# A hybrid decoder layer: the small on-chip tiles are allocated ahead of the staged block, not behind it

## The reference, cut to what matters

```python
h = x
proj = rmsnorm(h, norm_mix_g) @ w_in                      # 1024 -> 4624 columns
y_a  = gmlp_chunk_mixer(proj[..., :2048], ...)            # gelu, per-head norm, causal mixing in chunks of 128
y_b  = ssd_mixer(proj[..., 2048:], ...)                   # conv of 4 taps, silu, chunked state-space scan, gate, norm
h = h + concat([y_a, y_b]) @ w_out                        # 2048 -> 1024
hid = relu(rmsnorm(h, norm_mlp_g) @ w_ff1)                # 1024 -> 4096
h = h + (hid * hid) @ w_ff2                               # 4096 -> 1024
gate = sigmoid(rmsnorm(h, ple_norm_g) @ w_ple_gate)       # 1024 -> 1024
h = h + gate * (p @ w_ple_proj)                           # 256 -> 1024
out = rmsnorm(h, final_norm_g)
```

## Time and profile before

| what | value |
|---|---|
| median of 3 runs | 772.87 us (771.78 to 773.25) |
| the profiled execution, its own time | 771.78 us |
| its span, first to last instruction | 770.1 us |
| mean granted TensorE clock | 0.998 of full speed |
| busy share of the span: PE, PEld, DVE, ACT, POOL | 98%, 81%, 57%, 42%, 11% |
| moved by DMA | 81.88 MB, 106 GB/s over the span |

### The profile page before, as it was taken

The page is one execution under the profiler, slowest core; times in us unless marked ns, Lnnn a source line. Parts: engine busy times, 40 slices in busy tenths (PEclk is TensorE's granted clock), DMA queues, the critical chain, the costliest instruction groups (busy, mean ns, idle before and its releaser), DMA issues.

```text
span 770.1 us, 9090 instructions
## 1 busy us (share of the span) xinstructions
PE 757.4 (98%) x3492; PEld 623.7 (81%) x3492; DVE 436.1 (57%) x488; ACT 326.3 (42%) x456; POOL 87.4 (11%) x60
## 2 busy tenths in 40 slices
PE   8999999999999999999999999999999999999996
PEld 7888877887887888888888888888888888888885
DVE  5556894668569575547454443444444444446754
ACT  6525447645475812326443140413223140323556
POOL 1022210864562000000000000000000000000000
PEclk9999999999999999999999999999999999999999
DMA  9622323432422443123423232332323232332102
GB/s 334 191 83 83 109 79 119 133 109 87 161 82 83 144 157 136 42 69 108 127 93 110 82 110 96 95 107 84 109 82 109 82 100 96 102 120 82 47 0 110
DMA packets 35193, 81.88 MB, mean 106 GB/s; under 512 B 3924, under 2 KB 5592, under 8 KB 35160
## 3 DMA queue, kind: packets, MB, share of 16 engines
q1 hardware_dynamic: 33928, 77.20, 30.8%
q10 hardware_dynamic: 1232, 4.23, 1.7%
HBM read 79.28 MB, written 2.13 MB: 106 GB/s over the span
## 4 chain that ended last, share of the span: by engine, by line
PE 93%; DVE 3%; ACT 1%; issue 1%; DMA 1%; SPq 0%; ACTq 0%; DVEq 0%
PE acc L1122 29%; PE acc L1124 29%; PE acc L1123 29%; PE side L1184 3%; PE side L1277 2%; DVE w_lo L751 1%; PE side L1244 1%; DVE conv L948 1%; DMA gain<-in_norm_mix_g 1%; PE side L1284 1%; PE side L1272 1%; DVE h L937 0%; PE acc L1201 0%; ACT w_hi L431 0%; PE side L1224 0%
## 5 line engine op out<-in xcount | busy, mean ns | idle before, releaser
L1122 PE MATMUL acc<-w_hi,a_hi 128*128 128x512 f32 x512 | 204.2, 399 | 0.0
L1124 PE MATMUL acc<-w_hi,a_lo 128*128 128x512 f32 x512 | 199.7, 390 | 0.0
L1123 PE MATMUL acc<-w_lo,a_hi 128*128 128x512 f32 x512 | 199.3, 389 | 0.0
L431 ACT ACTIVATE w_hi<-w_raw 128x1024 fp32r<-128x1024 f32 (+1 forms) x128 | 130.2, 1036 | 145.5 <-PE acc L1124 143.3
L751 DVE TENSOR_TENSOR w_lo<-w_raw,w_hi 128x1024 fp32r<-128x1024 f32 (+1 forms) x128 | 166.1, 1298 | 45.0 <-ACT w_hi L431 44.3
L802 DVE TENSOR_TENSOR h<-h,acc 128x1024 f32<-128x1024 f32 x48 | 58.6, 1220 | 106.1 <-PE acc L1124 106.0
L1122 PEld LDWEIGHTS acc<-w_hi,a_hi 128*128 128x128 f32 x512 | 96.2, 188 | 21.0 <-issue 1.4
L1123 PEld LDWEIGHTS acc<-w_lo,a_hi 128*128 128x128 f32 x512 | 96.2, 188 | 20.7 <-issue 1.4
L1124 PEld LDWEIGHTS acc<-w_hi,a_lo 128*128 128x128 f32 x512 | 96.1, 188 | 20.4
L1122 PE MATMUL acc<-b_hi,w_hi 128*128 128x512 f32 x256 | 99.6, 389 | 0.0
L1123 PE MATMUL acc<-b_lo,w_hi 128*128 128x512 f32 x256 | 99.6, 389 | 0.0
(11 more groups left out here) (183 smaller groups left out, 818.7 us busy)
## 6 DMA issues: line engine op xcount, KB each, us to landing
w_raw<-in_w_ff SPq DMA_DIRECT2D x64, 512.0 KB, 3.5
w_raw<-in_w_in SPq DMA_DIRECT2D x36, 512.0 KB, 3.8
w_raw<-in_w_out SPq DMA_DIRECT2D x16, 512.0 KB, 3.4
h<-in_x SPq DMA_DIRECT2D x8, 512.0 KB, 4.3
seg<-cs_dram ACTq DMA_DIRECT2D x8, 512.0 KB, 3.8
w_raw<-in_w_ple_gate SPq DMA_DIRECT2D x8, 512.0 KB, 3.8
out<-y SPq DMA_DIRECT2D x4, 512.0 KB, 2.6
w_raw<-in_w_ple_proj SPq DMA_DIRECT2D x4, 256.0 KB, 2.6
```

The source lines that it names most:

```text
L431: act.activation(w_hi[:, half, 2 * p:2 * p + n, :], w_raw[:, p, 0:n, :], ACT.Copy).then_inc(hi_ready, 1)
L1122: pe.matmul(dst, st[0], mv[0], start=start, stop=False)
L1123: pe.matmul(dst, st[0], mv[1], start=False, stop=False)
L1124: return pe.matmul(dst, st[1], mv[0], start=False, stop=stop)
```

## The change

The 31 small permanent tiles are taken before the stacked block instead of after it. Nothing else is different: the same tiles with the same sizes and types, the same nesting inside the block, the same instructions, the same semaphores and the same order on each engine. Only the start addresses of the tiles of lines 66 to 120 are new.

```diff
--- before.py
+++ after.py
@@ -63,30 +63,6 @@
         y = sb("y", [P, NS, D])
         gain = sb("gain", [P, 2, D])
         tmp = sb("tmp", [P, 4, 512])
-        with ExitStack() as early:
-            conv = sb("conv", [P, 2, 512], where=early)
-            xs_t = sb("xs_t", [P, 2, 512], where=early)
-        p_hi = sb("p_hi", [P, 2, SEQ], F32R)
-        p_lo = sb("p_lo", [P, 2, SEQ], F32R)
-        with ExitStack() as early:
...
-        b_hi = sb("b_hi", [P, KT, SEQ], F32R)
-        b_lo = sb("b_lo", [P, KT, SEQ], F32R)
         ident = sb("ident", [P, P])
         upper = sb("upper", [P, P])
         after = sb("after", [P, P])
@@ -118,6 +94,30 @@
         m_ssq = sb("m_ssq", [P, 12])
         m_rms = sb("m_rms", [P, 12])
         m_rstd = sb("m_rstd", [P, 12])
+        with ExitStack() as early:
+            conv = sb("conv", [P, 2, 512], where=early)
+            xs_t = sb("xs_t", [P, 2, 512], where=early)
+        p_hi = sb("p_hi", [P, 2, SEQ], F32R)
+        p_lo = sb("p_lo", [P, 2, SEQ], F32R)
+        with ExitStack() as early:
+            with ExitStack() as first:
+                dtT = sb("dtT", [2 * R, SEQ], where=first)
+                dts = sb("dts", [P, 5, NS * R], where=first)
+            lm = sb("lm", [P, RG, P], where=early)
+            cbm = sb("cbm", [P, P], where=early)
+            bcT = sb("bcT", [P, 4, SEQ], where=early)
+            with ExitStack() as first:
+                wsT = sb("wsT", [P, GH, P], where=first)
+            b_nat = sb("b_nat", [P, G2, NS, P], where=early)
+            xdt = sb("xdt", [P, 512], where=early)
+            xdd = sb("xdd", [P, 512], where=early)
+            with ExitStack() as first:
+                wdt_hl = sb("wdt_hl", [P, KT, P], F32R, where=first)
+                wdt_h = sb("wdt_h", [P, KT, P], F32R, where=first)
+            seg = sb("seg", [P, 2, RG, P], where=early)
+            carry = sb("carry", [P, 512], where=early)
+        b_hi = sb("b_hi", [P, KT, SEQ], F32R)
+        b_lo = sb("b_lo", [P, KT, SEQ], F32R)
```

## The result

The changed kernel takes 778.94 us (median of 4 runs, 777.57 to 779.05) against 773.05 us for the kernel before (4 runs, 771.78 to 773.25). The ratio is 1.0077, with a 95% interval of 1.0064 to 1.0089: slower by 5.9 us, by the difference of the medians. That is above the 774.9 us at which my range ended, and about four times the 1.55 us that I called no change. In all 17 executions of the changed kernel that are on record it took 777.6 to 780.4 us. The executions of one kernel gather at two values about 1.3 us apart (771.8 and 773.2 us for the kernel before), so a median can fall on either, and the ratios, which are taken over whole sets of executions, are the better measure.

What follows compares the result with a forecast made beforehand. The prediction took PE's matmul count times a 226.7 ns step as the bound. All terms were 0, so 771.78 us stayed 771.8 for the profiled execution; it forecast the median, 772.9 us, range 770.9 to 774.9.

Steps and rivals of the forecast that it cites:

- What bounds the kernel: Whole kernel: PE is 93% of the chain, so time is the number of matmuls times their step, 226.7 ns.
- The addresses: Tile starts: small tiles move down 40,960 bytes, the stacked block up 6,592, to 64 bytes past multiples of 128.
- `b_hi` and `b_lo` as moving data: 0: 768 matmuls that move `b`: no change from starts 64 bytes past a multiple of 128; upper bound 10.9 us.
- `dA` row: Six 64-column matmuls on the worse-placed `dA`: 102 ns each against 108 on `xdt`, read as a worse start not being slower.
- The lower bound: Matmuls moving `b`: the fastest with `b_lo` is 1 ns under the median, 0.8 us in all.
- `b` and `p` as stationary data: 0: 432 loads of 188 ns, each under a 226.7 ns step with 39 ns to spare: no change, 3.6 us at most.
- The vector work: DVE and ACT on the moved tiles, such as the convolution taps at 746 to 748 ns: 0, at most 1.9 us.
- POOL: POOL's passes over `seg` and its landing: 0; growth of 5.5 us would be paid from 34.7 us of waiting.
- the small tiles: The small tiles keep their place relative to 256 bytes and have few, short instructions: 0, to a tenth of a us.
- The gain of 1.5%: Landing of `seg`: a row needs 130 beats and not 132 by the page's rule, under 0.1 us lower in the sum.
- The slower rival: Feed-forward blocks: PE reads in units that the new starts split, 14.5 us more, 787.4 to 789.3 us; 5 in 100.
- The faster rival: Convolution taps: vector engines reach the moved tiles quicker, at most 2.0 us less, to 770.9 us; 4 in 100.

Runs made afterwards that it cites:

- the run with 16 bytes: The kernel before with a_hi and a_lo read and written 16 bytes past their tile's start, b_hi and b_lo 240 bytes past it: 781.96 us in one run.

## Why the prediction was wrong, point by point

**What bounds the kernel** held. PE is still 93% of the chain and paces everything, so a few ns in its step went straight into the time.

**The addresses** were worked out rightly, but I looked at them one tile at a time. The large tiles that don't move were left out of the argument as unchanged. Their distance to `b` changed, and that is what costs.

**"`b_hi` and `b_lo` as moving data: 0" is the step that failed.** It measured 6.6 ns for each of 768 matmuls, 5.1 us, inside the bound of 10.9 that I gave and then set aside. I chose 0 by the `dA` row. That row shows a distance as well as a start (`dA` moving against a 128-column stationary tile 32 bytes off), but its matmuls have 64 columns and a step of 102 ns, and after the change it is what it was, 275 ns. A matmul too short to be paced by its columns says nothing on what paces 512 of them. I noted that this was open, and still gave the slower side only 5 in 100. The lower bound was misread as well: 388 ns stands in the row where `b_lo` is stationary, and where it moves all three values are 389.

**"`b` and `p` as stationary data: 0"** was off by less: 2.1 ns, 0.8 us, against a bound of 3.6. The load itself did not grow, 188 ns as before. The loss is in the step of the matmuls that move `w`. So the argument by the 39 ns to spare under the step was of the wrong kind.

**The vector work, POOL and the small tiles** held: taps of 746 to 749 ns in the groups by line, and POOL's passes and the landing of `seg` as before among the instructions that touch it. The landing's median is 3.8 us in both kernels. The gain of 1.5% that I held possible would be 0.06 us, too little to be seen there.

```profile
L948 DVE SCALAR_TENSOR_TENSOR conv<-acc,cols,conv 128x510 f32<-128x510 f32 x12 | 9.0, 749 | 0.4
```

```profile
L396 POOL TENSOR_TENSOR seg<-seg,cs x8: 1892/1894/1898, 133.9 to 226.3; 128x1024 f32<-128x1024 f32 x8
...
DMA to landing us min/median/max: 3.5/3.8/5.5
```

**The sign that I named beforehand** came as named, a step over 229 ns in FF1 with FF2 unchanged. The slower rival put the loss in the right stage, but with the wrong cause: the kernel with all tiles 64 bytes past a multiple of 128 is as fast as before. Its price of 14.5 us was more than double what the change costs. The faster rival did not occur.

No kernel tried is faster than the kernel before. The changed order with 64 bytes added, and the kernel before with all tiles shifted, are the same as it by their ratios of 0.9997 to 0.9999 (the widest interval reaches from 0.9987 to 1.0009).

## What to carry to other kernels

Where PE paces a kernel with matmuls like these (512 columns of this type, a weight load for each), keep the tiles that it loads and the tiles that it moves at starts that are equal modulo 256 bytes. A small tile taken between large ones can cost every matmul 1 to 3% of its step, and a pad brings it back. Such a loss shows in no wait and no clock: read the step between starts, stage by stage, and compare it between kernels. A row that is said to exclude a cost must have the same pacing as the instructions that would pay it.

## What the runs showed of the hardware that I had not expected

With 512 columns of this 4-byte type at the full clock, the step of a matmul is 226.7 ns (544 cycles) when the moving and the stationary tiles' starts are equal modulo 256 bytes. It is 229.0 ns at a distance of 64 and 232.5 to 234.2 at the other multiples of 32. The first number did not depend on the starts themselves, at three of them (0, 128 and 192 modulo 256). That the cause is a meeting of the two reads in the memory is an inference from this, not shown. For it speaks that the step follows the two starts together and neither alone, and that in FF1 of the changed kernel it is 233.3 ns in 248 of 249 threes, while the work of DVE and ACT comes and goes. Against a simple form of it stand the two runs with the low parts moved (with all low parts moved the threes of GATE take 227 ns and 237 ns in equal number, 30 and 30) and the run with 16 bytes, where the same two tiles run at 226.7 or 233.3 ns. No run took the weight loads out or changed the number of columns, so their part in it is untested.
